# A weight piece's remainder moved from DVE to POOL, and the overflow placing cut into thirteen parts

## The reference, cut to what matters

```python
def hierarchical_moe(xn, w_rg, b_rg, w_re, b_re, w_g, w_u, w_d):
    ...                                # group by top-1, then top-2 of its 4 experts: gates (512, 16)
    y = jnp.zeros_like(t)              # t: (512, 1024) normed tokens
    for e in range(N_EXPERTS):         # 16
        hid = jax.nn.silu(t @ w_g[e]) * (t @ w_u[e])     # w_g, w_u: (1024, 256)
        y = y + gates[:, e:e + 1] * (hid @ w_d[e])       # w_d: (256, 1024)
    return y.reshape(b, s_len, d)
```

## Time and profile before

| what | value |
|---|---|
| median of 3 runs | 1600.07 us (1598.69 to 1601.12) |
| the profiled execution's own time | 1602.11 us |
| its span, first to last instruction | 1599.9 us |
| TensorE busy | 1460.6 us (91%) |
| DVE busy | 931.6 us (58%) |
| ScalarE busy | 845.0 us (53%) |
| POOL busy | 446.9 us (28%) |
| mean granted clock of TensorE | 0.967 of full speed |
| expert stage of layer 0, of layer 1 | from about 612 and 1400 us to the layer's end |

### The profile page before, as it was taken

One profiled execution on the slowest core, in us unless ns is written; L12 is line 12 of the kernel. 1 busy time (PEld: TensorE's weight loads), 2 busy tenths in 40 slices (PEclk: granted clock), 3 DMA queues, 4 the chain that ended last, 5 costly groups with the idle time before them and its releaser, 6 DMA issues.

```text
span 1599.9 us, 22011 instructions
## 1 busy us (share of the span) xinstructions
PE 1460.6 (91%) x7636; PEld 1131.9 (71%) x7636; DVE 931.6 (58%) x1844; ACT 845.0 (53%) x1665; POOL 446.9 (28%) x634
## 2 busy tenths in 40 slices
PE   7999999999999995999689999999999999779993
PEld 5786777677767884777477867776677678667772
DVE  3544655534554446999654455645444535579995
ACT  4445555555443335888533555555554433558882
POOL 3314228320000025853005043284000000268210
PEclk9999999999999997999879999999999999989997
DMA  6822222112232366999566212221122332679995
GB/s 154 149 78 55 64 56 66 53 54 63 64 112 76 101 204 223 337 363 354 195 176 120 75 53 63 58 72 53 53 67 60 107 95 98 226 241 346 372 320 195
DMA packets 154325, 226.82 MB, mean 142 GB/s; under 512 B 20547, under 2 KB 89923, under 8 KB 154212
## 3 DMA queue, kind: packets, MB, share of 16 engines
q1 hardware_dynamic: 142724, 205.43, 42.2%
q0 software_dynamic: 10768, 17.80, 3.3%
q10 hardware_dynamic: 720, 2.16, 0.4%
HBM read 216.80 MB, written 25.49 MB: 151 GB/s over the span
## 4 chain that ended last, share of the span: by engine, by line
PE 67%; DVE 13%; issue 6%; ACT 5%; DMA 5%; POOL 3%; SPq 1%; ACTq 0%; POOLq 0%; DVEq 0%
PE bank L488 17%; PE bank L490 16%; PE bank L489 16%; PE bank L1399 4%; DVE xT L553 4%; PE bank L1384 3%; PE bank L1375 3%; PE bank L1377 2%; ACT xT L547 2%; DMA raw<-in_w_in_dram 2%; DVE oT L856 1%; POOL rsq L1970 1%; DMA rows<-ytok 1%; PE bank L1431 1%; PE bank L1434 1%
## 5 line engine op out<-in xcount | busy, mean ns | idle before, releaser
L488 PE MATMUL bank<-wh,xT 128*128 128x512 f32 (+1 forms) x960 | 401.5, 418 | 15.4 <-DVE xT L1743 5.3
L490 PE MATMUL bank<-wh,xT 128*128 128x512 f32 (+1 forms) x960 | 376.6, 392 | 0.0
L489 PE MATMUL bank<-wl,xT 128*128 128x512 f32 (+1 forms) x960 | 375.3, 391 | 0.0
L461 ACT ACTIVATE wh<-raw 128x512 fp32r<-128x512 f32 (+1 forms) x300 | 187.2, 624 | 330.1 <-PE bank L490 314.0
L467 DVE TENSOR_TENSOR wl<-raw,wh 128x512 fp32r<-128x512 f32 (+1 forms) x300 | 214.6, 716 | 245.8 <-ACT wh L461 235.1
L488 PEld LDWEIGHTS bank<-wh,xT 128*128 128x128 f32 x960 | 182.1, 190 | 83.3 <-issue 33.0
L490 PEld LDWEIGHTS bank<-wh,xT 128*128 128x128 f32 x960 | 181.7, 189 | 37.9
L489 PEld LDWEIGHTS bank<-wl,xT 128*128 128x128 f32 x960 | 182.9, 191 | 30.6 <-issue 1.4
L1542 ACT ACTIVATE prob<-prob,nmax 128x128 f32<-128x128 f32 (+3 forms) x192 | 107.2, 560 | 124.5 <-DVE nmax L1755 124.0
L1755 DVE CUSTOM_DVE_ANT_0 prob<-bank,mask 128x128 f32<-128x128 f32 (+3 forms) x128 | 60.6, 489 | 187.6 <-PE bank L1375 98.6
L2078 POOL TENSOR_TENSOR rows<-x_rows,ac 128x512 f32<-128x512 f32 x16 | 21.9, 1405 | 514.6 <-DVE x_rows L1826 514.6
(11 more groups left out here) (328 smaller groups left out, 2545.7 us busy)
## 6 DMA issues: line engine op xcount, KB each, us to landing
raw<-in_w_in_dram SPq DMA_DIRECT2D x192, 256.0 KB, 2.7
bqkv<-in_w_expert_gate_dram SPq DMA_DIRECT2D x64, 256.0 KB, 4.9
bqkv<-in_w_expert_up_dram SPq DMA_DIRECT2D x64, 256.0 KB, 6.0
bqkv<-in_w_expert_down_dram SPq DMA_DIRECT2D x32, 512.0 KB, 7.2
q_c<-in_w_expert_gate_dram SPq DMA_DIRECT2D x64, 256.0 KB, 5.4
q_c<-in_w_expert_up_dram SPq DMA_DIRECT2D x64, 256.0 KB, 6.8
head_odd<-in_w_expert_down_dram SPq DMA_DIRECT2D x32, 512.0 KB, 6.9
raw<-in_w_branch_dram SPq DMA_DIRECT2D x48, 256.0 KB, 2.6
```

The source lines that it names most:

```text
L461: nc.scalar.activation(wh[:, i % HL, 0:width], raw[:, i % RAW, 0:width], ACT.Copy).then_inc(hi_ready, 1)
L488: nc.tensor.matmul(out, lhs[0], rhs[0], start=start, stop=False)
L489: nc.tensor.matmul(out, lhs[0], rhs[1], start=False, stop=False)
L490: return nc.tensor.matmul(out, lhs[1], rhs[0], start=False, stop=stop)
```

## The change

The remainder of the sixth piece (j = 5) of experts 0 to 14 is made on POOL instead of DVE, and counted by a semaphore of its own, `last_lo_ready`; `pair_lo_ready` counts five pieces an expert. `pair_split` is the wait for either, on TensorE and on SP. (The sixteenth expert's two down pieces have other numbers and stay on DVE.) POOL's order becomes: the gathers of experts 0 to 3, and then for each expert e its sixth remainder, the gather for e+4, the scatter of e, one of thirteen parts of `place_overflow`, and two gain loads. The six parts before are cut into thirteen without another change of their operations. `overflow_table` goes from step 9 to 13 and `overflow_slots` from step 10 to 14. The declaration of the new semaphore is left out here.

```diff
...
@@ -362,7 +362,7 @@
             "small_copied": NT, "fz_dve": 6, "fz_act": 2, "csq_ready": 3 * NT, "csum_ready": 1, "c_ready": 1,
             "dve_own": len(PAIRS), "router_done": NT + 1, "logits_copied": NT, "r_act": 2, "r_mask": 1, "r_counted": 2, "r_addr": 2, "r_ctl": 1,
             "wr_split": 3, "r_pair": 1, "experts_const": 48, "xn_out": 16 * NT, "pair_hi_ready": 6 * NE,
-            "pair_lo_ready": 6 * NE, "pair_used": 3 * NE, "h_done": NE, "y_done": 2 * NE, "xg_turned": 2 * NE,
+            "pair_lo_ready": 5 * NE + 1, "last_lo_ready": NE - 1, "pair_used": 3 * NE, "h_done": NE, "y_done": 2 * NE, "xg_turned": 2 * NE,
             "xgT_hi": 2 * NE, "xgT_lo": 2 * NE, "th_ready": NE, "silu_half": NE, "hid_ready": NE, "hid_turned": NE,
             "hidT_hi": NE, "hidT_lo": NE, "x_first": NT, "x_done": NT, "rows_grown": 2 * NT, "rank_copied": 1,
             "r_ranked": 2, "r_table": 2}
@@ -510,6 +510,13 @@
         def pair_no(e, j):
             return j if is_const(e, -1) else 4 + 6 * e + j
 
+        def pair_split(eng, e, j):
+
+            if j == 5:
+                eng.wait_ge(last_lo_ready, of(last_lo_ready, e + 1))
+            else:
+                eng.wait_ge(pair_lo_ready, of(pair_lo_ready, (j if is_const(e, -1) else 4 + 5 * e + j) + 1))
+
         def pair_role(e, j):
 
             return 4 + j if is_const(e, NE - 1) else j
@@ -547,12 +554,12 @@
             nc.scalar.activation(pair_w[:, pair_ring(e, j, par), 0], pair, ACT.Copy).then_inc(pair_hi_ready, 1)
 
         def pair_lo(e, j, par, half):
+            eng, done = (nc.gpsimd, last_lo_ready) if j == 5 else (nc.vector, pair_lo_ready)
             pair, landed, count = pair_place(e, j, par, half)
-            nc.vector.wait_ge(pair_hi_ready, of(pair_hi_ready, pair_no(e, j) + 1))
-            nc.vector.wait_ge(landed, of(landed, count))
-            nc.vector.tensor_tensor(pair_w[:, pair_ring(e, j, par), 1], pair,
-                                    pair_w[:, pair_ring(e, j, par), 0].bitcast(F32),
-                                    ALU.subtract).then_inc(pair_lo_ready, 1)
+            eng.wait_ge(pair_hi_ready, of(pair_hi_ready, pair_no(e, j) + 1))
+            eng.wait_ge(landed, of(landed, count))
+            eng.tensor_tensor(pair_w[:, pair_ring(e, j, par), 1], pair,
+                              pair_w[:, pair_ring(e, j, par), 0].bitcast(F32), ALU.subtract).then_inc(done, 1)
 
         def load_gate_up(sp, expert, j, par, s_):
 
@@ -710,19 +717,15 @@
 
 
         def experts_sp(sp, layer):
-            def passed(value):
-
-                sp.wait_ge(pair_lo_ready, of(pair_lo_ready, value))
-
             def step(e, par, half):
 
                 if not is_const(e, 0) and not is_const(e, NE - 1):
                     for j in range(4):
-                        passed(j + 1 if is_const(e, 1) else pair_no(e - 2, j) + 1)
+                        pair_split(sp, -1 if is_const(e, 1) else e - 2, j)
                         load_gate_up(sp, layer * NE + (e + 1), j, 1 - par, pair_in[1 - par][j])
                 if not is_const(e, 0) and not is_const(e, 1):
                     for c in range(2):
-                        passed(pair_no(e - 2, 4 + c) + 1)
+                        pair_split(sp, e - 2, 4 + c)
                         load_down(sp, layer * NE + e, c, par, pair_in[par][4 + c])
 
             expert_steps(step)
@@ -770,18 +773,18 @@
             turn_chunk(0, 0, 0)
             turn_chunk(1, 1, 0)
             for j in range(4):
-                pe.wait_ge(pair_lo_ready, of(pair_lo_ready, j + 1))
+                pair_split(pe, -1, j)
                 gate_up(h_bank[0][:], xgT[0], pair_ring(-1, j, 1), j).then_inc(h_done if j == 3 else pair_used, 1)
 
             def step(e, par, half):
-                if e == 9:
+                if e == 13:
                     overflow_table()
                 for j in range(4):
                     if not is_const(e, NE - 1):
                         if j == 0:
                             pos_wait(pe, hid_ready, of(hid_ready, e))
                             pe.wait_ge(xgT_lo, of(xgT_lo, 2 * (e + 2)))
-                        pe.wait_ge(pair_lo_ready, of(pair_lo_ready, pair_no(e, j) + 1))
+                        pair_split(pe, e, j)
                         gate_up(h_bank[1 - par][:], xgT[1 - par], pair_ring(e, j, par), j)\
                             .then_inc(h_done if j == 3 else pair_used, 1)
                     if j == 1:
@@ -877,7 +880,7 @@
 
             def step(e, par, half):
                 end = is_const(e, NE - 1)
-                if e == 10:
+                if e == 14:
                     overflow_slots(dve)
                 if not end:
                     pair_lo(e, 3, par, half)
@@ -886,7 +889,6 @@
                     .then_inc(hidT_lo, 1)
                 if not end:
                     pair_lo(e, 4, par, half)
-                    pair_lo(e, 5, par, half)
                     silu(e + 1, 1 - par)
                     if not is_const(e, NE - 2):
                         rows_lo(e + 2, par)
@@ -927,19 +929,23 @@
                     pool.wait_ge(r_addr, of(r_addr, 2))
                 scatter(ysb[:, e % 2, :], home_i[:, e:e + 1], y_out[e % 2])
 
-            for e in range(NE):
+            def rows_of(e):
                 if e >= 2:
                     pool.wait_ge(xg_turned, of(xg_turned, 2 * (e - 1)))
                 gather(xg[:, e % 2, :], tab_i[:, e:e + 1], xg_in[e % 2])
-                if e >= 4:
-                    home(e - 4)
-                if 2 <= e < 8:
-                    place_overflow(pool, e - 2)
-                if e >= 4 and layer + 1 < DEPTH:
-                    for q in range(2 * (e - 4), min(N_GAINS, 2 * (e - 3))):
+
+            for e in range(4):
+                rows_of(e)
+            for e in range(NE):
+                if e < NE - 1:
+                    pair_lo(e, 5, e % 2, e // 2)
+                if e + 4 < NE:
+                    rows_of(e + 4)
+                home(e)
+                place_overflow(pool, e)
+                if layer + 1 < DEPTH:
+                    for q in range(2 * e, min(N_GAINS, 2 * e + 2)):
                         load_gain(pool, layer + 1, q)
-            for e in range(NE - 4, NE):
-                home(e)
             overflow_pool(pool)
 
         bounds = []
@@ -1082,6 +1088,7 @@
             cnt, ovc, extra, incl = (few[:, c, 8:] for c in range(4))
             row, chunk = (r1[:, d:d + 2, :].rearrange("p k n -> p (k n)") for d in (8, 10))
             m8 = 2 * NT
+            cmp = over_sum[0:1].rearrange("p k n e -> p (k n e)")[:, 0:n_ov * NE].rearrange("p (c e) -> p c e", c=n_ov)
             if part == 0:
                 pool.wait_ge(rank_copied, of(rank_copied, 1))
                 step(nc.gpsimd.memset(few[:, 3:5, :], 0.0))
@@ -1089,6 +1096,7 @@
                 for c in (2, 3):
                     step(ts(extra, cnt, float(c * P), None, ALU.is_gt))
                     step(tt(ovc, ovc, extra, ALU.add))
+            elif part == 1:
                 step(copy(incl, ovc))
                 for b, sh in enumerate((1, 2, 4, 8)):
                     s_, d_ = few[:, 3 + b % 2], few[:, 4 - b % 2]
@@ -1096,37 +1104,40 @@
                 step(tt(extra, incl, ovc, ALU.subtract))
                 step(tt(extra, extra, erow[:], ALU.subtract))
                 step(ts(extra, extra, float(NE - 1), None, ALU.add))
-            elif part == 1:
+            elif part == 2:
                 step(ts(over, rank, float(P), None, ALU.is_gt))
                 step(copy(q_, over))
                 for c in (2, 3):
                     step(ts(place, rank, float(c * P), None, ALU.is_gt))
                     step(tt(q_, q_, place, ALU.add))
+            elif part == 3:
                 step(tt(place, over, over_n(extra), ALU.mult))
                 step(tt(place, place, over_n(erow[:]), ALU.add))
                 step(tt(place, place, q_, ALU.add))
                 step(ts(q_, q_, -float(P), -1.0, ALU.mult, ALU.add))
                 step(tt(rank, rank, q_, ALU.add))
-            elif part == 2:
+            elif part == 4:
                 of_choices(8, rank)
+            elif part == 5:
                 of_choices(10, place)
-            elif part == 3:
+            elif part == 6:
                 for c in range(n_ov):
                     ins = ts(over_eq[:, :, c], chunk, float(NE + c), None, ALU.is_equal)
                 step(ins)
+            elif part == 7:
                 ts(over_tok[:, :, 0, :], over_eq, tok_id[:, 0:1], None, ALU.mult)
                 tt(over_tok[:, :, 1, :], over_eq, tile_no.unsqueeze(2).broadcast_to([P, m8, n_ov]), ALU.mult)
-                tt(over_tok[:, :, 2, :], over_eq, home_no.unsqueeze(2).broadcast_to([P, m8, n_ov]), ALU.mult)
-            elif part == 4:
-                for m in range(m8):
+                step(tt(over_tok[:, :, 2, :], over_eq, home_no.unsqueeze(2).broadcast_to([P, m8, n_ov]), ALU.mult))
+            elif part in (8, 9, 10):
```

(13 more changed lines are left out.)

## The result

The changed kernel took 1632.2 us in the median of four runs (1624.75 to 1634.68), beside 1599.68 for the kernel before on the same chip (1598.69 to 1601.12): ratio 1.0195, with a 95% interval of 1.0159 to 1.0231, so 32.5 us slower. The profiled execution took 1634.68 us (span 1632.9, against 1599.9 before). All but about 2 us of it is in the two expert stages, and the loop forecast is there, but it costs more in layer 0 than the 19.5 us that I had put there.

The account below looks back on a forecast made before the run. DVE, TensorE and ScalarE are nearly full in 10.25 us expert steps; moved work closes a loop through POOL. Terms 15.4+0.4+2.6+1.9+3-0.6 = 22.7 us on 1602.11 profiled, forecast 1623 against the 1600.07 median; range 1599 to 1648.

Parts of the forecast that it names:

- The loop through POOL: Expert stages: POOL's remainder, second down group, output copy, scatter, part, gain loads and next remainder wait for one another.
- The undisturbed step: Expert step with POOL in time: 9.95 us instead of 10.25, with ScalarE late next.
- The price on POOL: POOL's 128x1024 remainder takes 2.4 us, bounds 1.9 and 2.6.
- Who may read SBUF: Expert stages: POOL operations and DVE's two-SBUF-input remainders exclude one another; POOL's 8-element addition takes 1.10 us instead of 0.20.
- Step = s + 3.95: The next expert step can't begin before 3.95 us after s, the start of POOL's remainder counted from the step's start.
- The loop through the scatter, +2.6, and a part of 3.9: POOL's scatter ends 2.6 us into the next step; the overflow part behind it takes 3.9 us, bounds 1.9 and 5.0.
- Steps behind parts and gain loads, 11 x 1.40: Layer 0: eleven steps of 11.65 us, remainder starting at +7.7, cost 15.4 us.
- Layer 1, 13 x 0.2: Layer 1: thirteen steps behind a part alone, 10.45 us each, cost 2.6 us.
- Two or three steps beyond +8.5, 3 us: Steps whose remainder on POOL would start beyond +8.5 wait 1.2 us more for DVE's first remainder: 3 us.
- Rival C: POOL's remainder regularly held out by several DVE remainders in eleven gain-load steps: 2.5 us more each, 27 in all, 1650; chance 0.12.
- The end of each stage, 0.95: Last expert but one: its second down group begins 0.95 us later in each layer, 1.9 in all.
- Rival A: Faster: POOL has room, remainder 1.9 us and part 2.2, all steps 9.95, total -7.5 us, 1593; chance 0.13.

Follow-up runs that it names:

- experiment 2: Changed kernel with the overflow placing and its table left out, the sixth remainder still on POOL: 1592.75 us, 0.995 of the kernel before.
- experiment 5: Changed kernel with gain loads before the scatter, and the scatter one expert behind (e-1 instead of e): 1610.29 us, 1.0059 of the kernel before.
- experiment 4: Changed kernel with 16 spare 128x128 products on TensorE before the second down group, layer 0 steps 1 to 10: 1627.11 us, 1.0164 of the kernel before.
- experiment 11: Changed kernel with POOL's remainder for experts 8 to 13 only, six parts in steps 0 to 5, gain loads first: 1603.01 us, 1.0008 of the kernel before.
- experiments 8 and 9: Changed kernel with six dependent 128x64 additions (1636.0 us, one run) or six such memsets (1590.37 us, one run) in place of the overflow placing.
- experiment 10: Changed kernel with POOL's remainder for experts 6 to 13 only, six parts in steps 0 to 5, gain loads first: 1619.42 us, 1.011 of the kernel before.

## Why the prediction was right in sign and short in size

Forecast was 1623 (22.7 us more by the sum), measured 1632.2, 32.5 more. The loop through POOL was forecast and is there; what the sum lacks is TensorE's clock. Term by term:

- **The undisturbed step, 9.95.** Right: 9.90 in experiment 2, with POOL's remainder waiting for ScalarE's leading half.
- **The price on POOL, 2.4 us.** Right: 2.39. The 2.3 estimated from the Trainium skill's figure (GPSIMD Engine Reference, section Performance versus the Vector engine) was also near.
- **Who may read SBUF.** The reading holds, with one slip: DVE's remainder at 58.92 ends 0.55 us behind POOL's operation of 58.68 to 59.72, not 0.69. The least that such a remainder takes is 548 ns, so that it waited for POOL's end fits even better.
- **Step = s + 3.95.** Right: s + 4.0 in every step with the clock at its upper level, but for one in each layer (s + 4.2), behind which the overflow table's eight products stand.
- **The loop through the scatter, +2.6, and a part of 3.9.** Both sizes right (+2.61; parts take 3.0 to 4.5 us in layer 1, 3.8 in the mean). But the loop is not the only one: experiment 5 took it away and layer 1's steps with long parts stayed. I had priced the exclusion and not seen that DVE's remainders move along with POOL's.
- **Steps behind parts and gain loads, 11 x 1.40.** s was 7.85 in the mean of these eleven (6.16 to 8.58) against 7.7: with 4.0 behind it, 11.85 a step instead of 11.65, some 2 us more in all.
- **Layer 1, 13 x 0.2.** The mean step was 10.62 and not 10.45: 4.8 us instead of 2.6. Most of the difference is one step (1476.80, 12.06 us, s = 8.11); the other twelve are 10.50 in the mean. Its part took only 2.96 us, but its scatter came late and ended at +5.04 instead of +2.6. The scatter of the same expert is late in layer 1 of the kernel before too (1451.70, behind 3.88 us of "issue", also 1.74 us long); what holds it stays open:

```profile
1480.10 1.74 POOL L715 DMA_INDIRECT ytok<-ac,prob  x1 [2.82 <-issue]
```

- **"Two or three steps beyond +8.5, 3 us."** Not there. Only two steps came to such an s (8.53, 8.58) and the remainder of 8.58 started at once and took 2.38 us; it was DVE's next that was held out. Rival C, built on the same mechanism, did not happen for that reason.
- **The end of each stage, 0.95.** The size was right and partly by luck. The last output copy of a stage comes 1.01 us (layer 0) and 0.94 us (layer 1) later behind the last gate/up group than before. But the last remainder on POOL took 3.14 and 3.10 us, held out for 0.7 by one of DVE's, which I had not put there; and something behind it does absorb: the second down group of the last expert but one begins 1.37 us later in layer 0, and 1.0 of that is left at the end. In experiment 2, where that remainder takes 2.48 us, the ends cost 0.5 each.
- **The term that was missing.** I took TensorE's clock as given, since it is 1.00 in the earlier trace rows. The change makes TensorE stand still for up to 2.77 us right before the second down group. Six times in layer 0 the clock then fell, over the group, over the end of it and the next step's first products, or (from 729.0 on) mostly over those. Seven steps have a granted clock of 0.87 to 0.90, an eighth 0.97. The eleven steps take 136.2 us, where 11 x (s + 4.0) is 130.4: 5.8 us, and 4.4 by experiment 4, whose remainders started 0.18 us later each.

In sum, layer 0's stage lost 25.0 us against 19.5, layer 1's 5.9 against 3.3 (each instruction of ScalarE in the one trace set beside its like in the other). That layer 0 came out only 5.5 us off is partly luck: the 3 us for late remainders, which did not come, cover half of the 5.8 us of the clock. The remaining 2 us are between the stages, in the attention of layer 1, which moves by 2.2 us in experiment 11 and 0.8 in experiment 2 in the same direction; I can't tell it from noise.

Rival A (POOL has room) is true of either half of the change, and false for both together: what I put against it, that each small operation that meets a remainder takes over 1 us, is what experiments 8 and 9 show.

## What to carry to other kernels

Before work goes to an engine that looks idle, follow its queue once around: count what stands between the event that it waits for and the operation that others will wait for, at the durations it has while the neighbour holds the shared access, and not by its busy share. An engine whose lateness was free pays for all its backlog in the first step in which somebody waits for it (that step took 21.8 and 17.4 us instead of 10.25 in experiment 10). And when a new wait falls on TensorE, price the products after it at the lower clock as well as at the upper; six of them cost 1.2 us more here.

## What the runs showed of the hardware that I had not expected

- TensorE's clock fell during or just behind waits of 1.96 to 2.47 us between busy groups, in some steps and not in others: the step of 651.45 has a wait of 2.77 us and a granted clock of 1.00, the next one 2.44 us and 0.88, and one of 2.26 us in layer 1 passed at 1.00. So the length of a single wait did not decide it. With 1.9 us of small products in the wait the clock stayed at 1.00 in all of these steps.
- The exclusion goes by reads. POOL's memset took 0.15 to 0.2 us under DVE's remainders; an addition of the same size took 1.16 instead of 0.30. Indirect gathers and scatters are held out as well: in the stages' steps the gather takes 1.0 to 1.1 us in the kernel without parts and up to 2.15 in the kernel after, where it begins under a remainder of DVE (the one at 1487.41 took 1.91 us, and the remainder ran until 0.94 us behind its start).
